# Token tiles in groups of four, three and one for the products by w_o

## The reference

```python
    y = hybrid_mixer(h, ...)                       # its last step: return o @ w_o, w_o is (1024, 1024)
    x = layer_norm(ALPHA * x + (1.0 + gt_a) * y, ln1_g[l], ln1_b[l])
    h = x * (1.0 + sc_f) + sh_f
    y = conv_ffn(h, ffn_w_up[l], ffn_conv[l], ffn_conv_b[l], ffn_w_down[l])

def conv_ffn(h, w_up, conv_w, conv_b, w_down):     # w_up is (1024, 5632), the convolution has 3 taps
    u = causal_dwconv(h @ w_up, conv_w) + conv_b
    gate, val = jnp.split(u, 2, axis=-1)
    return (jax.nn.silu(gate) * val) @ w_down
```

## Time and profile before

| | us |
|---|---|
| median of three runs | 3037.67 (3035.82 to 3041.81) |
| profiled execution, its own time | 3035.15 |
| its span, first to last instruction | 3033.6 |
| PE busy | 2859.8 (94%) |
| DVE busy | 1612.7 (53%) |
| ACT busy | 1013.5 (33%) |
| POOL busy | 790.8 (26%) |

### The profile page before, as it was taken

How to read it: one execution, slowest core, us unless ns; L and a number is a source line. 1 busy time by engine, 2 the same in 40 slices (tenths; PEclk the granted TensorE clock), 3 DMA queues, 4 the chain that set the end, 5 groups by cost and what they waited for, 6 DMA issues and landing times.

```text
span 3033.6 us, 33367 instructions
## 1 busy us (share of the span) xinstructions
PE 2859.8 (94%) x13340; PEld 2236.1 (74%) x13340; DVE 1612.7 (53%) x2537; ACT 1013.5 (33%) x1575; POOL 790.8 (26%) x456
## 2 busy tenths in 40 slices
PE   6998888999979999999999999999989999999998
PEld 3676556776647888888886778788757888888886
DVE  7545655553575555455557565776444333333335
ACT  2446532233212222222224750565454212222112
POOL 2322112221224444444451113311011222222221
PEclk9999999999999999999999999999999999999999
DMA  7211012222321211111112112013211111111111
GB/s 256 82 33 29 7 56 77 77 84 96 120 83 49 76 49 49 49 49 49 49 49 97 62 50 86 16 31 120 89 36 42 56 49 49 49 49 49 49 49 56
DMA packets 199768, 193.60 MB, mean 64 GB/s; under 512 B 16167, under 2 KB 147647, under 8 KB 199615
## 3 DMA queue, kind: packets, MB, share of 16 engines
q1 hardware_dynamic: 197984, 187.09, 19.5%
q10 hardware_dynamic: 1631, 4.40, 0.4%
HBM read 175.43 MB, written 13.89 MB: 62 GB/s over the span
## 4 chain that ended last, share of the span: by engine, by line
PE 77%; DVE 10%; ACT 7%; issue 3%; POOL 1%; DMA 1%; ACTq 0%; DVEq 0%; SPq 0%; POOLq 0%
PE bank L1315 62%; PE bank L1660 2%; PE bank L1422 1%; PE bank L1463 1%; PE bank L1644 1%; PE bank L1477 1%; PE bank L1612 1%; PE bank L1308 1%; DVE ffn_conv L2308 1%; PE bank L1428 1%; DVE ffn_conv L2304 1%; PE bank L1631 1%; PE bank L1679 0%; PE bank L1408 0%; POOL panel_lo L3065 0%
## 5 line engine op out<-in xcount | busy, mean ns | idle before, releaser
L1315 PE MATMUL bank<-ft_hi,panel_lo 128*128 128x512 f32 x1312 | 467.4, 391 | 1.7 <-DVE ftx_lo L1958 1.7
L3065 POOL TENSOR_TENSOR panel_lo<-panel,panelm_hi 128x1024 fp32r<-128x1024 f32 x64 | 153.3, 2396 | 577.0 <-ACT panelm_hi L2623 531.6
L1315 PEld LDWEIGHTS bank<-ft_hi,panel_lo 128*128 128x128 f32 x1312 | 247.0, 188 | 54.1 <-issue 2.8
L1315 PE MATMUL bank<-ft_hi,panel_hi 128*128 128x512 f32 x704 | 274.0, 389 | 0.0
L1315 PE MATMUL bank<-ft_lo,panel_hi 128*128 128x512 f32 x704 | 273.9, 389 | 0.0
L2304 DVE TENSOR_SCALAR ffn_conv<-ffn_in,ffn_taps 128x512 f32<-128x512 f32 x88 | 114.1, 1296 | 278.8 <-ACT ffn_in L2894 278.7
L2574 DVE TENSOR_TENSOR resid<-resid,bank 128x512 f32<-128x512 f32 x256 | 174.7, 687 | 151.5 <-PE bank L1315 150.7
L3065 POOL TENSOR_TENSOR panel_lo<-panel,panel_hi 128x1024 fp32r<-128x1024 f32 x66 | 157.9, 2401 | 244.3 <-ACT panel_hi L2623 231.1
L1315 PE MATMUL bank<-ft,panel 128*128 128x512 f32 x416 | 197.2, 613 | 7.4 <-ACT v_feat L2771 3.4
L1315 PE MATMUL bank<-ftm_hi,panelm_hi 128*128 128x512 f32 x512 | 200.6, 392 | 2.4 <-DVE ftm_lo L1958 2.4
L1315 PE MATMUL bank<-ftm_lo,panelm_hi 128*128 128x512 f32 x512 | 200.2, 391 | 0.0
(11 more groups left out here) (497 smaller groups left out, 6124.7 us busy)
## 6 DMA issues: line engine op xcount, KB each, us to landing
panel<-in_w_in SPq DMA_DIRECT2D x52, 512.0 KB, 3.9
panel<-in_w_ada SPq DMA_DIRECT2D x48, 512.0 KB, 3.8
panel<-in_ffn_w_up SPq DMA_DIRECT2D x44, 512.0 KB, 3.7
panel<-in_w_mlp_in SPq DMA_DIRECT2D x32, 512.0 KB, 3.9
panel<-in_w_mlp_out SPq DMA_DIRECT2D x32, 512.0 KB, 3.6
panel<-in_w_o SPq DMA_DIRECT2D x24, 512.0 KB, 3.6
panel<-in_w_out SPq DMA_DIRECT2D x24, 512.0 KB, 3.5
panel<-in_ffn_w_down SPq DMA_DIRECT2D x22, 512.0 KB, 3.6
```

Source lines behind the costliest of these rows:

```text
L1315: m = te.matmul(ps, a, b, start=(start and j == 0), stop=(stop and j == len(pairs) - 1))
L3065: pool.tensor_tensor(lo, k.view(p), hi.bitcast(F32), ALU.subtract).then_inc(*g.new("halved_lo", p))
```

## The change

The groups of the products by w_o become (0, 1, 2, 3), (4, 5, 6) and (7,). The first group's features (f1) use banks 6 and 7, since the second group now takes banks 0 to 5 for its sums; the last group takes banks 6 and 7. The feature steps of the second group (f2) move: the first stands behind the sixth panel of the last group, the second behind the seventh, and the two others behind the eighth, behind the norm and xhat of tile 7; the row products of tiles 4, 5 and 6 follow them there. Behind the splits of w_up come the features of tile 7 and its row product, and its row addition comes where that of tiles 6 and 7 was. The order in which DVE empties banks (mixed) follows the groups, and SP's load of mem waits for tile 7's features.

```diff
-    f1, a1 = feats(1, (0, 1, 2, 3), (4, 5)), applies(1, (0, 1, 2, 3))
-    f2, a2 = feats(1, (4, 5), (4, 5)), applies(1, (4, 5))
-    f3, a3 = feats(1, (6, 7), tuple(range(8))), applies(1, (6, 7))
+    f1, a1 = feats(1, (0, 1, 2, 3), (6, 7)), applies(1, (0, 1, 2, 3))
+    f2, a2 = feats(1, (4, 5, 6), (4, 5)), applies(1, (4, 5, 6))
+    f3, a3 = feats(1, (7,), tuple(range(8))), applies(1, (7,))
     grouped_products(k, "w_o", d["w_o"][0], 8, {
         (0, 7): [lambda: norm_start(k, 1, (0, 1, 2, 3)), *a1],
         (1, 2): f1[0:1], (1, 3): f1[1:2], (1, 4): [f1[2], *rows((0, 1))], (1, 5): [f1[3], *rows((2, 3))],
-        (1, 7): [lambda: norm_start(k, 1, (4, 5)), *a2],
-        (2, 4): f2[0:1], (2, 5): f2[1:2], (2, 6): [*f2[2:4], *rows((4, 5))],
-        (2, 7): [lambda: norm_start(k, 1, (6, 7)), *a3]}, split=True, made=made, plain=(1, 2))
+        (1, 7): [lambda: norm_start(k, 1, (4, 5, 6)), *a2],
+        (2, 5): f2[0:1], (2, 6): [*f2[1:2]], (2, 7): [lambda: norm_start(k, 1, (7,)), *a3, *f2[2:4], *rows((4, 5, 6))]},
+                     groups=((0, 1, 2, 3), (4, 5, 6), (7,)), banks=(tuple(range(8)), (0, 1, 2, 3, 4, 5), (6, 7)), split=True,
+                     made=made, plain=(1, 2))
...
     for step in f3:
         step()
-    for step in rows((6, 7)):
+    for step in rows((7,)):
         step()
     for n in range(2):
         up(0, n, first[n], 0)
-    k.unit("rows_add", 1, (6, 7))
+    k.unit("rows_add", 1, (7,))
...
-    mixed = [(h, n) for tiles in GROUPS for h in range(HALVES) for n in tiles]
+    mixed = [(h, n) for tiles in ((0, 1, 2, 3), (4, 5, 6), (7,)) for h in range(HALVES) for n in tiles]
...
-        if n < 6:
+        if n < 7:
             rows_add(s, (n,))
...
-        sp.wait_ge(*sp.filled("feat", 1, 6, KD - 1))
+        sp.wait_ge(*sp.filled("feat", 1, 7, KD - 1))
```

## The result

| | before | after |
|---|---|---|
| median (range), 20 runs each | 3035.93 us (3033.64 to 3042.01) | 3042.69 us (3036.04 to 3047.95) |
| profiled execution | 3035.15 | 3042.71 |
| its span, mean granted clock | 3033.6, 0.979 | 3041.3, 0.977 |

The ratio of after to before is 1.0018, with a 95% interval of 1.001 to 1.0025: slower by some 5.4 us (3 to 8), the ratio itself within the 0.2% that the prediction calls no change. The time lies in the prediction's range for 8 in 10 (3034 to 3045), and 0.7 us above the forecast's own range (3037 to 3042).

The account below looks back on a forecast made before the run. It took TensorE (PE) to bound the kernel, so its idle time counts: +4.0 - 2.7 = +1.3 us, with PE's late start +2, on 3037.67 gives 3039.7 us; own range 3037 to 3042, 8 in 10 3034 to 3045.

Parts of the forecast that it names:

- hole of PE ahead of it: Before the transposes of tiles 4 to 6, PE waits for xhat, idle 867.9 to 873.3: a new 5.4 us hole.
- clock behind it falls, costs: After the 5.4 us hole the clock falls to 1.2 GHz; what follows is about 2 us later.
- second hole: PE's waits of 2.83 and 0.88 us near 961, first feed-forward block; claimed filled, clock kept, 2.7 us back.
- The rival without a fall of the clock: Clock stays up at 868, everything behind 2 us earlier: -0.7 us, about 3037 us; chance 0.10.
- the one with the rows setting the pace: DVE rows fall behind POOL's low parts; tile 6's addition ends after 905, +6.5 us, 3044.2 us; chance 0.15.
- the shorter tail: Tile 7's earlier xhat reaches the first convolution, at 905; splits start before 891; -6.7 us, 3031 us; chance 0.07.
- a third of 7.24 us behind 893.52: Start of w_up on PE: released by POOL's first low part, at 895.9 before, some 5 us later after.
- the interleaving: DVE's remaining row work and POOL's low parts exclude each other; tile 6's 2.4 us shift POOL's end to 908.0.
- +1.3 from the chain: Chain reaches the second hole 4.0 us later, less 2.7 us given back by the clock there.
- PE's late start: PE begins w_up some 5 us later, at a low clock at first; may bind by 0 to 1.5 us.

Follow-up runs that it names:

- warm, first hole: Changed kernel plus six plain 512-column products on PE ahead of the transposes of tiles 4 to 6; ratio to the kernel before 1.0013.
- the late row of tile 6: Changed kernel with tile 6's row product and addition moved behind the features of tile 7; ratio to the kernel before 1.0009.
- order only: Kernel before with its groups of four, two and two kept; two feature steps and row products of tiles 4 and 5 moved behind the last norm; ratio 1.0002.
- the last kernel: Changed kernel with tile 6's row product behind tile 7's features and six plain products in PE's first hole; ratio to the kernel before 1.0000.
- the kernel with the splits freed: Kernel before with waits ahead of the first three w_up splits cut to their own buffers' users, and POOL not waiting for tile 7's xhat; ratio 1.0029.

## Why the prediction was right, and where it was not

**The moments.** On the prediction's scale:

| step | predicted | measured |
|---|---|---|
| xhat of tiles 4 to 6 done | 874.6 | 874.6 (877.26 + 2.26 - 4.92) |
| hole of PE ahead of it | 5.4 us | 5.30 us |
| clock behind it falls, costs | 2 us | 2.0 us (warm, first hole) |
| xhat of tile 7 done | 888.4 | 888.6 |
| rows of tiles 4 to 6 begin | 892.5 | 892.6 |
| splits on ACT | 896.9 | 896.95 |
| POOL's low parts | 898.1 to 908.0 | 898.1 to 907.1 |
| PE begins w_up | 900.5 to 901.8 | 902.97 |
| first convolution | 913.2 | 912.1 |
| second hole, its slow clock | gone | gone |

Counting each instruction through its queue held to a few tenths of a microsecond up to the start of POOL's low parts, 85 us behind the start of the second group; PE's start of w_up came 1.2 to 2.5 us later than forecast and the first convolution 1.1 us earlier. The count held since every duration had a row of the same shape or one between two shapes. The rival without a fall of the clock is refuted by the panel of 3.49 us, the one with the rows setting the pace by the addition of tile 6, which ended at 902.5 on that scale, under the 905 from which it decides, and the shorter tail by the splits' start. The Trainium skill's rule in "SBUF — State Buffer" (Who interferes with whom) agrees with what was measured: 3.25 us for an addition that takes 1.22, and 9.05 us for low parts that take 7.06 when no row work is beside them.

**What was missed** is the step "PE, which now can begin the products of w_up a third of 7.24 us behind 893.52": I let PE be released by POOL's low part alone, before and afterwards. Before, the first low part was ready at 895.9 and PE went on transposing until 896.47, where w_up follows without a wait; the bank of the first feature chunk had been empty since about 894.5. Afterwards there is a second condition, a bank that DVE has to empty, and the emptying is queued behind the addition that POOL stretches. It costs 1.5 us behind the end of the low part, and 2.45 us with the stretching of the low part itself, as the late row of tile 6 shows. The prediction named the interleaving and counted it only for the convolution behind it. So it followed DVE, while the chain of after is PE's from 907.89.

**The sum.** Forecast were +1.3 from the chain and up to 1.5 for PE's late start, +2 in all. The stage measured +1.3 against the profile that the sum was made from, and +2.0 (202.5 less 200.5) against the two later ones of the same kernel. By PE's account against that first profile: it begins w_up 6.50 us later (90.13 less 83.63), has the clock at 0.85 for 10.10 us where it was 1.00 (1.5 us), and is given back 2.83 + 0.88 us of idle time and some 2.7 us of low clock: 8.0 less 6.4, +1.6, of which 1.3 is measured. Against the third profile it is 4.70 us later (90.13 less 85.43), loses 1.0 us more to the clock (0.85 against 0.95 over those 10.10 us), and is given back 2.25 + 1.18 us: +2.3, of which 2.0 is measured. So the 2.7 us that the sum gives back at the second hole were taken from a single execution, and two of three do not have them. In the same two, w_up begins 1.8 us later, since they lose 1.7 us to a slow stretch in the second group which no profile of the changed kernel has (last section); the sum has no such term. That the two nearly make up for each other is luck, and so is a part of how near 3039.7 is to 3042.69 us: the forecast was put on 3037.67, the median of three runs, and the median of 20 is 3035.93. As a difference, 5.4 us (4.2 over all runs) was measured where +2 was forecast and +1 to +4 had a chance of 0.68.

**What stays open.** All runs together, 42 of the changed kernel with a mean of 3041.6 us and 137 of the kernel before with 3037.3, differ by 4.2 us (95%: 3.1 to 5.4, from the scatter of the runs). The stage explains 1.3 to 2.4 of them. By set of runs timed side by side, the means differ by 5.4, 4.3 and, in the third, 1.8 us (95%: -0.2 to 3.7), so the third set taken alone leaves nothing to explain. The rest was looked for behind the stage and isn't there as a fixed amount: it was 2021.0, 2021.0 and 2018.8 us after against 2019.5, 2019.7 and 2020.1 before. Ahead of it nothing is changed, and three profiles a kernel can't tell whether the 0.91 of the window from 400 to 500 comes more often in one. The same is to be seen in the order only and in the last kernel, whose stages and ratios don't keep step by 1 to 2 us. I leave some 2 us unexplained; that places of low clock elsewhere lie differently once the stage is shifted was not tested by a run, and neither was whether the slow stretch of the second group, in two of three profiles of the kernel before, is as frequent in its runs.

## What to carry to other kernels

When a start moves, list all that the first instruction waits for, and its banks too, and ask for each who empties it and what is queued in front of that; a condition that was slack by a microsecond or two (here the bank, emptied 2 us early) may be the one that ends last. An engine that stands waiting can be doing another a service: before a wait is cut, look whether the work behind it excludes what the other engine does at that time. A few plain products in a hole of PE give back what the clock takes only if the hole is really filled (5.30 us: gained 2.0 us; 10.22 us with six products, 4.91 us left idle: gained nothing). And a stretch of low clock that a sum gives back or leaves out should be looked for in a second profile of the same kernel.

## What the hardware did that was not expected

- Two engines that exclude each other lose on both sides: three low parts 9.05 and 9.89 us instead of 7.06, four row instructions 9.46 instead of 5.28.
- A kernel's own executions differ by fixed steps at one place (the kernel before: 812.8, or 817.2 and 818.9 us at the second group, with 0.95 or 0.91 of the clock between 400 and 500), and this scatter is as large as what the change costs.
- In the kernel before, the profiles differed at the stage itself. In the second group PE waits four times, 2.5 us in all, for xhat of tiles 0 to 3; behind that the later two profiles have a slow stretch which the first has not. The third profile:

```profile
829.07 0.30 PE L1308 MATMUL bank<-ident,xhat 128*128 128x128 f32 x1 [1.37 <-DVE xhat L1918]
829.70 0.33 PE L1308 MATMUL bank<-ident,xhat 128*128 128x128 f32 x1 [0.33 <-DVE xhat L1918]
830.42 0.33 PE L1308 MATMUL bank<-ident,xhat 128*128 128x128 f32 x1 [0.39 <-DVE xhat L1918]
831.15 0.76 PE L1308 MATMUL bank<-ident,xhat 128*128 128x128 f32 x5 [0.40 <-DVE xhat L1918]
831.75 5.29 PE L1315 MATMUL bank<-panel,mixed 128*128 128x512 f32 x8
```

The same eight records take 3.60 us in the first profile, after waits of the same length. So w_up began at 85.4 instead of 83.6. The order only and the kernel with the splits freed had the stretch as well: four of five profiles with two tiles in the second group. With three tiles PE comes to these transposes 15.45 us behind the group's start (833.21 less 817.76), when xhat of tile 3 is done (13.84), so it doesn't wait, and none of the eight profiles has the stretch. So the change gives back up to 1.7 us here, which the prediction has no term for and no run tested by itself.
- The load of mem of those two profiles was nevertheless 0.7 us earlier (200.5 against 201.25): the second hole was there (2.25 and 1.18 us in the third profile), but no slow stretch followed it, as the third profile's windows around and behind it show:

```profile
969.00:981.00 12.00, 10.25 (x44) 8.18 (x45) 10.03 (x17) 3.05 (x5) 4.77 (x2) 1.00 0.13 45
981.00:988.40 7.40, 7.40 (x35) 6.12 (x33) 1.95 (x3) 1.06 (x1) 2.39 (x1) 1.00 0.24 71
```

The 2.7 us that the prediction let the change give back there are lost in one of three executions of the kernel before, and not in the other two.
